# Modulation vectors of a two-block transformer: running sums on VectorE and GpSimd in place of matmuls on TensorE

## The reference, cut to what matters

```python
silu_c = jax.nn.silu(c)
silu_cc = jax.nn.silu(c_ctx)
for l in range(DEPTH):
    last = l == DEPTH - 1
    mod_l = silu_c @ w_mod[l] + b_mod[l]
    mod_c = silu_cc @ w_mod[l] + b_mod[l]
    sh_l, sc_l, g_l = jnp.split(mod_l, 3, axis=-1)
    sh_c, sc_c, g_c = jnp.split(mod_c, 3, axis=-1)
    h_l = rmsnorm(x, norm_g[l]) * (1 + sc_l[:, None]) + sh_l[:, None]
    h_c = rmsnorm(ctx, norm_g[l]) * (1 + sc_c) + sh_c
    ...
    x = x + g_l[:, None] * y_l
    if not last:
        ctx = ctx + g_c * y_c
return rmsnorm(x, final_g)
```

## Time and profile before

| | |
|---|---|
| median of 3 runs | 1082.8 us (1082.21 to 1083.21) |
| the profiled execution, from its first to its last instruction (span) | 1082.7 us |
| PE busy | 1054.7 us, 97% |
| DVE busy | 682.7 us, 63% |
| ACT busy | 553.5 us, 51% |
| POOL busy | 77.7 us, 7% |
| mean granted clock of PE | 0.995 of full |

### The profile page before, as it was taken

One profiled execution on the slowest core, in us unless ns is written; L12 is line 12 of the kernel. 1 busy time (PEld: TensorE's weight loads), 2 busy tenths in 40 slices (PEclk: granted clock), 3 DMA queues, 4 the chain that ended last, 5 costly groups with the idle time before them and its releaser, 6 DMA issues.

```text
span 1082.7 us, 15600 instructions
## 1 busy us (share of the span) xinstructions
PE 1054.7 (97%) x5974; PEld 884.7 (82%) x5974; DVE 682.7 (63%) x1201; ACT 553.5 (51%) x1002; POOL 77.7 (7%) x95
## 2 busy tenths in 40 slices
PE   7999999999999999999999999999998999999997
PEld 6899777788887999777688778899996678889785
DVE  5985666666546895675667448433456744976664
ACT  6664365555436564364555445334335733544772
POOL 1000110000002000110000000001000002120040
PEclk9999999999999999999999999999999999999999
DMA  9644586766666655586876584233231021542001
GB/s 328 212 142 155 181 262 201 252 209 183 192 194 229 218 156 156 162 296 190 286 234 180 182 318 133 71 93 108 79 95 40 1 78 40 156 155 98 2 1 40
DMA packets 109844, 170.73 MB, mean 158 GB/s; under 512 B 7245, under 2 KB 70746, under 8 KB 109514
## 3 DMA queue, kind: packets, MB, share of 16 engines
q1 hardware_dynamic: 107668, 161.95, 47.2%
q0 software_dynamic: 1568, 6.37, 1.8%
q10 hardware_dynamic: 534, 1.41, 0.3%
HBM read 168.19 MB, written 1.05 MB: 156 GB/s over the span
## 4 chain that ended last, share of the span: by engine, by line
PE 88%; DVE 5%; ACT 2%; DMA 2%; issue 2%; SPq 1%; POOL 0%; DVEq 0%; POOLq 0%; ACTq 0%
PE PS L482 17%; PE PS L487 16%; PE PS L483 16%; PE PS L3038 4%; PE PS L3042 4%; PE PS L3039 4%; PE PS L989 2%; PE PS L1838 2%; PE PS L1949 1%; PE PS L950 1%; PE PS L951 1%; PE PS L955 1%; PE PS L1826 1%; PE PS L1776 1%; DMA raw<-w_gate_up 1%
## 5 line engine op out<-in xcount | busy, mean ns | idle before, releaser
L452 DVE TENSOR_TENSOR low<-raw,high 128x1024 fp32r<-128x1024 f32 (+3 forms) x182 | 202.2, 1117 | 175.0 <-ACT high L442 173.9
L482 PE MATMUL PS<-high,hT_high 128*128 128x512 f32 (+2 forms) x796 | 303.0, 381 | 0.3 <-ACT high L442 0.3
L483 PE MATMUL PS<-high,hT_low 128*128 128x512 f32 (+2 forms) x796 | 295.8, 372 | 0.0
L442 ACT ACTIVATE high<-raw 128x1024 fp32r<-128x1024 f32 (+3 forms) x186 | 179.4, 972 | 218.8 <-PE PS L487 123.7
L487 PE MATMUL PS<-low,hT_high 128*128 128x512 f32 (+2 forms) x796 | 231.7, 372 | 1.2 <-DVE low L455 1.2
L482 PEld LDWEIGHTS PS<-high,hT_high 128*128 128x128 f32 x796 | 150.2, 189 | 34.1 <-issue 9.3
L487 PEld LDWEIGHTS PS<-low,hT_high 128*128 128x128 f32 x796 | 147.4, 188 | 23.8 <-DVE low L455 2.8
L483 PEld LDWEIGHTS PS<-high,hT_low 128*128 128x128 f32 x796 | 150.4, 189 | 19.3
L455 DVE SCALAR_TENSOR_TENSOR low<-raw,vec_cols,high 128x512 fp32r<-128x512 f32 x176 | 123.6, 747 | 66.4 <-ACT high L445 66.3
L445 ACT ACTIVATE high<-raw,vec_cols 128x512 fp32r<-128x512 f32 x176 | 117.1, 715 | 62.8 <-PE PS L487 31.1
L3038 PE MATMUL PS<-high,fT_high 128*128 128x512 f32 x176 | 69.5, 395 | 0.0
(11 more groups left out here) (376 smaller groups left out, 1603.0 us busy)
## 6 DMA issues: line engine op xcount, KB each, us to landing
raw<-w_gate_up SPq DMA_DIRECT2D x176, 256.0 KB
raw<-w_mod SPq DMA_DIRECT2D x48, 512.0 KB
raw<-w_down SPq DMA_DIRECT2D x44, 512.0 KB
raw<-w_in SPq DMA_DIRECT2D x56, 384.0 KB
raw<-o_w_in SPq DMA_DIRECT2D x20, 512.0 KB
raw<-w_out SPq DMA_DIRECT2D x16, 512.0 KB
raw<-e_w_in SPq DMA_DIRECT2D x12, 512.0 KB
raw<-w_in SPq DMA_DIRECT2D x8, 512.0 KB
```

The costliest lines, as they stand in the source:

```text
L442: last = e.activation(g.high, g.raw, ACT.Copy)
L452: last = e.tensor_tensor(g.low, g.raw, g.high.bitcast(F32), ALU.subtract)
L482: e.matmul(bank, xh[:, k, tokens], g.high[:, i, :], start=first and i == 0, stop=False)
L483: e.matmul(bank, xl[:, k, tokens], g.high[:, i, :], start=False, stop=False)
```

## The change

A modulation granule is now one block of 128 rows and 1024 columns (`add_mod(layer, third, k)`). Since silu(c) of a row is one number per partition, a block's share is block times that number: VectorE keeps a running sum of the eight blocks for LAT in `mod_sum[:, 0]`, GpSimd one for CTX in `mod_sum[:, 1]`. When both are complete, TensorE sums over the partitions with a vector of ones: into four strips for the first two thirds, which are then copied (`mod_rows`), transposed, and read as columns; into all 128 partitions at once for the gates. The gate's bias is no longer in these columns: a DMA brings it to all partitions and GpSimd adds it to `post_gain`. For the gates of the last layer GpSimd alone keeps the one sum that is needed.

The blocks stand elsewhere in the ring: the first third in gate/up chunks 1 to 8 of each layer, the second in the down product, one in every two granules, the third of layer 0 beside the even layer's q and kv weights, the third of layer 1 as eight blocks in a row behind the even layer's output weights. `stats`, `sink` and `k_pe` move into the constants' tile, which is why the rows below name `consts` for them.

```diff
-        MOD_AT = {(2, 1): (0, 0), (2, 3): (0, 2), (4, 1): (1, 0), (4, 3): (1, 2)}
-        def add_mod(layer, third, cs=(0, 1), pairs=PAIRS):
+        def add_mod(layer, third, k):
             ph = w_mods.setdefault((layer, third), Phase(f"mod{third}"))
-            for c in cs:
-                for rows in pairs:
-                    ph.add(a["w_mod_2"][layer], rows, D * third + 512 * c, 512, cut=False)
-        MOD_LAST = (4, 5, 7, 8)
+            ph.add(a["w_mod_2"][layer], (k,), D * third, D, cut=False)
+        MOD_CHUNKS, MOD_DOWN = range(1, 9), range(1, 17, 2)
...
             for n in range(FK):
-                if last and n in MOD_LAST:
-                    c, half = divmod(MOD_LAST.index(n), 2)
-                    add_mod(layer, 2, (c,), PAIRS[2 * half:2 * half + 2])
+                if n - 3 in MOD_DOWN:
+                    add_mod(layer, 1, MOD_DOWN.index(n - 3))
                 w_down[layer].add(a["w_down"][layer], (n,), 0, D)
...
         e_out = [late_phase(f"e_out{c}", "e_w_out_2", PAIRS, 512, 512 * c) for c in range(2)]
+        for k in range(DK):
+            add_mod(1, 2, k)
...
-                    sp.wait_ge(mods_done, before.mod + 1)
+                    sp.wait_ge(mods_ctx, before.mod + 1)
+                    if before.mod <= w_mods[0, 2].last.mod:
+                        sp.wait_ge(mods_lat, before.mod + 1)
...
+        def mod_lat_dve(e, g):
...
+            if k == 0:
+                mod_sum_free(e, g)
+                e.tensor_scalar(mod_sum[:, 0, :], g.raw[:, 0, :], silu_c[:, 0, 0:1], None, ALU.mult).then_inc(mods_lat, 1)
+            else:
+                e.scalar_tensor_tensor(mod_sum[:, 0, :], g.raw[:, 0, :], silu_c[:, 0, k:k + 1], mod_sum[:, 0, :],
+                                       ALU.mult, ALU.add).then_inc(mods_lat, 1)
+        def mod_pool(e, g, s, part):
...
+            if k == 0:
+                mod_sum_free(e, g)
+                e.tensor_scalar(mod_sum[:, s, :], g.raw[:, 0, :], silu_c[:, s, 0:1], None, ALU.mult).then_inc(mods_ctx, 1)
+            else:
+                e.tensor_scalar(part, g.raw[:, 0, :], silu_c[:, s, k:k + 1], None, ALU.mult).then_inc(pool.sem, pool.mark(f"mod_part{g.mod}"))
+                e.wait_ge(pool.sem, pool.value(f"mod_part{g.mod}"))
+                e.tensor_tensor(mod_sum[:, s, :], mod_sum[:, s, :], part, ALU.add).then_inc(mods_ctx, 1)
+        def mod_sums_pe(e, third, bank):
+            mod_summed(e, w_mods[where.layer, third].last)
+            for s in range(2):
+                for c in range(2):
+                    at = 32 * (2 * s + c)
+                    last = e.matmul(PS[at:at + 32, bank, :], ones[:, 0:1].broadcast_to([P, 32]), mod_sum[:, s, 512 * c:512 * (c + 1)],
+                                    start=True, stop=True)
...
         def gates_pe(e, layer, streams, free):
+            mod_summed(e, w_mods[layer, 2].last, layer == 0)
             for s in streams:
...
+                for c in range(2):
+                    free(2 * s + c)
+                    last = e.matmul(PS[:, 2 * s + c, :], ones[:, 0:1].broadcast_to([P, P]), mod_sum[:, s, 512 * c:512 * (c + 1)], start=True, stop=True)
...
         def late_pool(e):
             norm_pool(e, "e_lat")
+            gate_bias_load(e, 0, late_bias)
+            for g in w_mods[0, 2].granules:
+                mod_pool(e, g, CTX, late_part)
+            for s in range(2):
+                gate_bias_pool(e, 0, s, late_bias)
...
             k_pe_spread_pool(e)
+            for g in w_mods[1, 2].granules:
+                mod_pool(e, g, LAT, mod_sum[:, 1, :])
+            e.wait_ge(mods_ctx, w_mods[1, 2].last.mod + 1)
+            gate_bias_load(e, 1, mod_sum[:, 1, :])
             e.wait_ge(pe.sem, pe.value(f"mla_scores{len(mla_steps) - 1}"))
             e.dma_start(ctx_now, a["ctx_2"].rearrange("b (t p) n -> b p t n", p=P)[0]).then_inc(s_ctx_again, 16)
...
                     cuts.to(w_gu[layer].granules[4 * c + h], 3)
-                    if h == 1 and c == 7:
-                        mod_take_dve(e, 0)
+                    if h == 1 and c in MOD_CHUNKS:
+                        mod_lat_dve(e, w_mods[layer, 0].granules[MOD_CHUNKS.index(c)])
...
                 cuts.to(w_down[layer].granules[min(n + 3, FK - 1)])
+                if n in MOD_DOWN:
+                    mod_lat_dve(e, w_mods[layer, 1].granules[MOD_DOWN.index(n)])
...
+                if n == 16:
+                    if layer == DEPTH - 1:
+                        e.wait_ge(dve.sem, dve.value("e_ctx_F0"))
+                    mod_sums_pe(e, 1, 0)
```

More of the change, by code:

```diff
@@ L474, in to @@
                     self.cut(self.e, cut_order[self.next])
+                    self.beside(self.e, cut_order[self.next])
                     self.next += 1
@@ L1008, in mod_take_dve @@
[L1008 to L1015 removed]
+        MOD_ORDER = ((0, 0), (0, 1), (1, 0), (1, 1), (0, 2), (1, 2))
@@ new lines, in mod_take_dve @@
+        def mod_take_dve(e, third, bank):
+            e.wait_ge(pe.sem, pe.value(f"mod_columns{third}"))
+            at = where.layer * 24 + 8 * third
+            bias = vec_cols[:, V_BM + at:V_BM + at + 8].rearrange("p (c b) -> p c b", c=2)
+            rows = PS[:, bank, :].rearrange("p (b s c r) -> p s c b r", b=4, s=2, c=2)
+            for s in range(2):
+                last = e.tensor_tensor(modT[:, at:at + 8, s].rearrange("p (c b) -> p c b", c=2), rows[:, s, :, :, 0],
+                                       bias, ALU.add)
@@ L1433, in mod_gain_dve @@
         def mod_gain_dve(e):
-            for layer in range(DEPTH):
-                ng = vec_cols[:, V_NG + layer * DK:V_NG + (layer + 1) * DK]
-                last = e.scalar_tensor_tensor(mod_gain[:, layer, :, :].rearrange("p s k -> p k s"),
-                                              modT[:, layer * 24 + DK:layer * 24 + 2 * DK, :], 1.0,
-                                              ng.unsqueeze(2).broadcast_to([P, DK, 2]), ALU.add, ALU.mult)
-            last.then_inc(dve.sem, dve.mark("mod_gain"))
+            layer = where.layer
@@ L2618, in pool_layer @@
             if layer + 1 < DEPTH:
+                for third in range(2):
+                    for g in w_mods[layer, third].granules:
+                        mod_pool(e, g, CTX, mod_part[:, :])
                 boundary_pool(e, "ffn", layer)
             else:
+                for g in w_mods[layer, 0].granules:
+                    mod_pool(e, g, CTX, mod_part[:, :])
                 e.wait_ge(granules_done, w_gu[DEPTH - 1].granules[3].cut + 1)
@@ L2626, in pool_layer @@
                 norm_pool(e, "e_ctx")
+                for g in w_mods[layer, 1].granules:
+                    mod_pool(e, g, CTX, mod_part[:, :])
                 for t in range(NT):
@@ L2644, in _, with boundary_act @@
             late_pool(e)
-        def boundary_act(e, side, layer, cuts, banks, granules, x_banks, third):
+        def boundary_act(e, side, layer, cuts, banks, granules, x_banks):
             output_squares_act(e, side, 0, banks)
@@ L2923, in turn_x_t1, with boundary_pe @@
             return lambda: x_turn_pe(e, side, 1, banks, lambda j: e.wait_ge(dve.sem, dve.value(f"{side}_x1{'' if j else 'a'}")), layer)
-        def boundary_pe(e, side, layer, last_four, output, x_banks, granules, name, third):
+        def boundary_pe(e, side, layer, last_four, output, x_banks, granules, name):
             for t in range(NT):
```

269 lines of the change are left out of this document (124 added, 145 removed).

## The result

The changed kernel takes **1108.8 us** (median of four, 1107.6 to 1113.2) against 1082.8, a ratio of 1.0246 (95% interval 1.0233 to 1.0258). The direction was forecast, and so were the two places where most of it is lost; the size was not: +25.9 us measured, +8.1 forecast. 1108.8 lies inside the stated range of 1071 to 1113, but above the forecast's own 1080 to 1102.

A forecast was written before the change was run, and what follows sets the result against it. TensorE, busy 97% of the span, was taken as the bound. -25.4 + 5 + 3 + 12 + 1.5 + 1.5 + 10.5 = +8.1 on 1082.7 gave about 1091 us, range 1071 to 1113 (own range 1080 to 1102).

The forecast's parts named there:

- TensorE's gain: TensorE, whole kernel: 31.0 us of matmuls removed, 5.6 added, a net gain of 25.4 us.
- The step that failed: GpSimd's price for scaling one 128x1024 block: between 1.2 and 2.38 us, taken as 1.2, so 3.6 a block.
- Rival 2: GpSimd's TENSOR_SCALAR costs as much as its TENSOR_TENSOR, 2.38 us: +24, 1115 us; chance 0.13.
- Layer 1's down: Down projection of layer 1: 44.7 us of GpSimd and VectorE work in 32.6, so TensorE waits 12 us.
- End of the even layer: Late last blocks delay the context reload, so TensorE waits 10.5 us (8 to 15) at its turn.
- Gate/up: Gate/up chunks of both layers, eight blocks each: 2.5 us lost a layer, 5 in all.
- Layer 0's down: Down projection of layer 0: 9.3 us too much work, the cuts' lead covers 6, 3 us lost (0 to 10).
- Even layer's input: GpSimd starts the next set just when VectorE splits the normed input: 1.5 us lost (0 to 4).
- Attention: Three blocks in the wait for the spread of keys, a fourth beside VectorE work: 1.5 us lost (0 to 5).
- The seam: Between the layers, two removed matmul blocks hid a VectorE chain: of 3.7 us, some 1.6 gained, 2.1 not.
- They exclude each other: GpSimd and VectorE instructions with all inputs in SBUF each wait for the other's whole instruction, so their times add.

The follow-up runs named there:

- e11: Changed kernel with all running sums on VectorE and the context reload issued as soon as the scores are done: 1060.8 us.
- e1: Changed kernel with GpSimd's scaling cut to 512 of 1024 columns and the sum adding the block itself (result not correct): 1094.5 us.
- e9: Changed kernel with GpSimd's root of the context's norm behind the third of its eight blocks in layer 1's down projection: 1092.1 us.
- e3: Changed kernel with the context reload ahead of the last four of GpSimd's eight blocks behind the output weights: 1100.6 us.
- e7: Changed kernel with all running sums on VectorE, the context reload still behind GpSimd's wait for the last sum and bias load: 1073.8 us.

## Why the prediction was right in sign and wrong in size

**TensorE's gain: right.** Forecast -25.4; e11 shows -28.4 up to the end of the attention and -23.5 in all. Of the 4.7 us given back in e11 at the end of the even layer, 3.3 are waits for the turns (1.2 and 2.8 us, where before had 0.7); the forecast had no term for them. The 2.8 stands in the changed kernel too, and its rows name the cause. There:

```profile
957.83 3.45 DVE L2073 TENSOR_SCALAR qT<-kT,consts 128x1024 f32<-128x1024 f32 x1 [0.66 <-POOL consts L2063]
958.37 2.36 POOL L1490 TENSOR_TENSOR post_gain<-post_gain,mod_sum 128x1024 f32<-128x1024 f32 x1
961.39 1.94 PE L772 MATMUL PS<-consts,qT 128*128 128x128 f32 x16 [2.79 <-issue]
```

L1490 is the bias add that the change gave GpSimd. Beside it VectorE's scaling of the second tile, 0.75 us in the kernel before, lasts 3.45, and TensorE's turn waits for that scaling. The forecast had no term for the bias add.

**The step that failed** is "TENSOR_SCALAR [...] not below half, 1.2, and not above the whole, 2.38; I take 1.2, and 3.6 us for a block". The upper bound came from counting inputs: one input, so not dearer than two. It measured 2.85, and a block 5.2 us. The point is not the pick within the bounds but the bounds: an operation of which no row exists is not bounded by a row of another form. e1, with 1.57 us for it, takes 14.3 of the 18.0 us away that the kernel lies above the forecast. Rival 2 (1115 us) was the nearest, and by luck: its price was still too low, and by its own working 2.85 instead of 1.2 adds 24 x 1.65 / 1.2 = 33 us, which makes 1124 (an estimate). The forecast had a second error of the other sign, that the engines exclude each other for the whole of every such instruction; see below. The Trainium skill (GPSIMD Engine Reference, Engine selection) calls a one-input operation roughly line rate on this engine; the trace says 2.5 ns a column here, and 2.85 us against the 2.34 us of the two-input sum, and the measurement decides.

**Layer 1's down: 12 forecast, 18.0 of wait and 21.3 in all.** GpSimd's chain, in the changed kernel's trace (start us, us):

```profile
604.12 0.73 POOL L735 TENSOR_TENSOR consts<-consts,half_power 128x2 f32<-128x2 f32 x1 [48.42 <-DVE consts L753]
604.86 2.85 POOL L1011 TENSOR_SCALAR mod_sum<-raw,silu_c 128x1024 f32<-128x1024 f32 x1
...
651.76 5.89 POOL L1015 TENSOR_TENSOR mod_sum<-mod_sum,mod_part 128x1024 f32<-128x1024 f32 x1
```

The root came 14.6 us behind TensorE's first matmul (589.56), as the forecast had it (616.3 - 601.84 = 14.5). From 604.86 to 657.65 are 52.8 us where 44.7 were forecast. GpSimd's own part is 8 x 2.85 + 7 x 2.35 = 39.3 instead of 26.3, 13.0 more, and that is the price. The rest is 13.5 instead of 18.4: 11.7 in which its instructions last longer beside VectorE's, and 1.8 of gaps between them. It is less since VectorE can run through the later part of a TENSOR_SCALAR. 3.5 of it fall on the last sum (5.89 instead of 2.35), on which TensorE waits: VectorE ran five two-input instructions in a row, up to 655.46, before that sum ended at 657.65. Four of them are the context's split (L815), which the forecast did not count:

```profile
651.84 1.28 DVE L815 TENSOR_TENSOR cT_low<-xn,cT_high 128x512 fp32r<-128x512 f32 x2
...
654.18 1.28 DVE L815 TENSOR_TENSOR cT_low<-xn,cT_high 128x512 fp32r<-128x512 f32 x2
```

TensorE wanted the sums at 639.75, 50.2 us in, where the forecast had 47.1. Most of the rest of 21.3, beside the wait of 18.0, is the low clock behind it:

```profile
625.00:650.00 25.00, 14.75 (x74) 12.09 (x72) 21.61 (x16) 7.73 (x10) 24.07 (x8) 0.84 0.59 212
650.00:675.00 25.00, 17.20 (x71) 12.86 (x72) 11.71 (x19) 8.34 (x14) 8.13 (x3) 0.75 0.46 161
```

The last number but two is the granted clock, 0.84 and 0.75 around a wait of 18 us, where the kernel before has 1.00: a mean of stretches at the full 2.4 GHz and, from the idle time on, at the lower 1.2 GHz. From 657.8, where TensorE goes on, to about 662.4 its matmuls start 0.43 us apart instead of 0.23. The forecast had no term for that. And e9 adds what the forecast had named but not priced: the place of the root alone is worth 16.6 us with GpSimd's scaling at 2.85. While it stood in front, the first block held its slot, and no load was issued between 593.03 and 607.74. e1 takes 9.4 us off this stretch and e9 16.5, together more than its 21.3, so price and place are not two separate shares of it.

**End of the even layer: 10.5 forecast, 16.0 measured.** In before's time plus the 7.9 us of shift, the last block was to end at 916.0 and did at 920.3 (the price again: GpSimd became the bound, with no wait for data between its last blocks); the reload took 7.9 instead of 6.5; the adds 5.4 instead of 5.1; the turn came at 940.4, not 935.0. A wait of 3.0 for the last sum in front of the gates (L1480), the second wait of 2.8 and a clock of 0.73 in 925 to 950 us were not in the sum. The price alone does not explain this term: in e1 the last sum ends at 898.98, within about 1 us of the forecast's time, and the stretch still costs 15.5, since the reload takes 10.8. e3 shows the reload's share (8.2), e11 that of the 12.6 only 1.2 is left when the blocks are VectorE's and the reload goes out early.

**The smaller terms.** Gate/up 5: measured 2.0 at the end of layer 0's (TensorE waits 2.1 us for the columns of modT) and nothing in layer 1. Layer 0's down 3: 4.4 (2.8 of it the wait for VectorE's sum). Even layer's input 1.5: 1.1. Attention 1.5: 2.9. The seam: from the first matmul of layer 0's down to the end of the seam e11 gains 0.7 us, where the forecast's terms make 1.9.

**They exclude each other: right for one of GpSimd's two forms, and over-counted for the other.** Beside a TENSOR_TENSOR on GpSimd, a VectorE instruction whose inputs are all in SBUF is held until that ends, unless GpSimd's is itself still waiting (651.84 above). One with a PSUM operand is not held, as the forecast took it (L2919, 0.68 us beside one and elsewhere). In the changed kernel, VectorE's first running sum of layer 0's down, with one SBUF input, lasts 2.89 us instead of the 0.75 that it takes undisturbed, and ends 0.55 behind GpSimd's:

```profile
273.08 2.83 POOL L1015 TENSOR_TENSOR mod_sum<-mod_sum,mod_part 128x1024 f32<-128x1024 f32 x1
273.56 2.89 DVE L992 TENSOR_SCALAR mod_sum<-raw,silu_c 128x1024 f32<-128x1024 f32 x1
```

The Trainium skill (SBUF — State Buffer, Who interferes with whom) counts such a tensor_scalar in a two-port mode among those that exclude GpSimd; the forecast had no row for it, and this one agrees: 2.89 instead of 0.75. The same section says of the two-port modes that whoever issues first has the ports "for the whole instruction". For L2073 above the trace differs: its record starts 0.54 us before that of GpSimd's L1490, and it is the one held. For GpSimd's TENSOR_SCALAR the trace differs too. VectorE's L452 below started 0.28 us into one that lasted from 604.86 to 607.71, and was done at 607.05, after 1.91 us, 0.7 more than alone; L761, with one SBUF input, took 0.85 more than 0.75 and was done at 616.06, inside one that ended at 617.25:

```profile
605.14 1.91 DVE L452 TENSOR_TENSOR low<-raw,high 128x1024 fp32r<-128x1024 f32 x1 [1.11 <-ACT high L442]
...
614.46 1.60 DVE L761 TENSOR_SCALAR e_ctx_normed<-ctx_raw,consts 128x1024 f32<-128x1024 f32 x1
...
618.32 3.42 DVE L452 TENSOR_TENSOR low<-raw,high 128x1024 fp32r<-128x1024 f32 x1
```

while the last, beside a TENSOR_TENSOR, had to wait for its end. It fits that the gate/up chunks and layer 0's down cost 6.4 us in all, where the forecast had 8 for a scaling of less than half the true length.

## What to carry to other kernels

Bound the price of an operation that no row shows by what would follow if it were dearer than its nearest relative, not by an argument about its inputs; here 48 scalings at 2.85 instead of 1.2 us turned a small loss into a large one (with 1.57, in e1, 11.5 us over the kernel before; with 2.85, 25.9). Before giving a slow engine new work in program order, look at what it already waits for: a root in front of eight blocks became worth 16.6 us, and a reload behind them 8.2 (13.0 behind a wait for the last sum, in e7). And work in which two engines hold each other off can be better given whole to the faster one, where that one has room: with both sums on VectorE (busy 74%) and GpSimd free, the same change takes 1060.8 us, 2.1% less than before.
